# Low halves of the weights from glu to mix, written by accumulating transfers

## The reference

```python
h = rmsnorm_2(x, norm1_g)
z = h @ w_in + b_in
z_glu, z_rx, z_rg, z_ga, z_gb = jnp.split(z, split_idx, axis=-1)
u = z_glu[..., :D_CONV] * jax.nn.sigmoid(z_glu[..., D_CONV:])
u = causal_depthwise_conv(u, conv_dw_w, conv_dw_b)        # 31 taps, 1024 channels
u = jax.nn.silu(layernorm(u, conv_ln_g, conv_ln_b))
y_a = u @ conv_w_out + conv_b_out
xb = causal_depthwise_conv(z_rx, lru_conv_w, lru_conv_b)  # 4 taps, 1280 channels
hb = rg_lru(xb, ...)                                      # gates (two block matrices), then a scan in time
y_b = (hb * jax.nn.gelu(z_rg, approximate=True)) @ lru_w_out
m = jax.nn.sigmoid(z_ga) * y_a + jax.nn.sigmoid(z_gb) * y_b
x = x + m @ w_mix_out
h = rmsnorm_2(x, norm2_g)
x = x + (jax.nn.silu(h @ ffn_w1) * (h @ ffn_w3)) @ ffn_w2
```

## Time and profile before

| | us |
|---|---|
| median of 3 runs | 1075.47 |
| lowest, highest | 1074.18, 1077.63 |
| the profiled execution, its own time | 1070.71 |
| its span, first to last instruction | 1068.8 |
| TensorE matmul busy | 1003.8 (94%) |
| VectorE busy | 788.7 (74%) |
| ScalarE busy | 524.7 (49%) |
| GpSimd busy | 1.9 |

### The profile page before, as it was taken

One profiled execution on the slowest core, in us unless ns is written; L12 is line 12 of the kernel. 1 busy time (PEld: TensorE's weight loads), 2 busy tenths in 40 slices (PEclk: granted clock), 3 DMA queues, 4 the chain that ended last, 5 costly groups with the idle time before them and its releaser, 6 DMA issues.

```text
span 1068.8 us, 20025 instructions
## 1 busy us (share of the span) xinstructions
PE 1003.8 (94%) x7906; PEld 944.9 (88%) x7906; DVE 788.7 (74%) x1449; ACT 524.7 (49%) x823; POOL 1.9 (0%) x14
## 2 busy tenths in 40 slices
PE   4659999999999889999999999999989999999996
PEld 1259999999888779999999989998868999999995
DVE  4477678887767468778766779899995787777554
ACT  3236575444655356666445435457215564444341
POOL 0000000000000000000000000000000000000000
PEclk9679999999999999999999999999999999999998
DMA  9978585888548646555465535363434556555531
GB/s 377 421 319 315 180 313 178 303 329 330 182 124 294 239 161 247 186 173 194 158 223 182 180 108 213 119 236 119 158 118 142 216 174 217 179 179 192 197 119 40
DMA packets 35943, 222.76 MB, mean 208 GB/s; under 512 B 3819, under 2 KB 9116, under 8 KB 9500
## 3 DMA queue, kind: packets, MB, share of 16 engines
q1 hardware_dynamic: 35868, 221.71, 57.8%
HBM read 220.62 MB, written 1.07 MB: 207 GB/s over the span
## 4 chain that ended last, share of the span: by engine, by line
PE 81%; DVE 10%; ACT 3%; DMA 3%; issue 1%; SPq 0%; DVEq 0%; ACTq 0%
PE bank L557 23%; PE bank L559 23%; PE bank L558 23%; PE bank L798 6%; PE bank L848 3%; DVE y L1560 2%; DMA mod_raw<-w_mod 2%; DVE w_lo L1242 1%; PE bank L576 1%; DMA raw<-weights 1%; DVE rt L1623 1%; DMA x<-x_in 0%; PE bank L602 0%; ACT w_hi L909 0%; PE bank L724 0%
## 5 line engine op out<-in xcount | busy, mean ns | idle before, releaser
L557 PE MATMUL bank<-xg_hi,w_hi 128*128 128x258 f32 (+1 forms) x1264 | 360.9, 286 | 4.6 <-DVE w_lo L1242 2.8
L1242 DVE TENSOR_TENSOR w_lo<-raw,w_hi 128x1024 fp32r<-128x1024 f32 x270 | 326.6, 1217 | 45.7 <-ACT w_hi L909 44.8
L558 PE MATMUL bank<-xg_lo,w_hi 128*128 128x258 f32 (+1 forms) x1264 | 356.7, 282 | 0.0
L559 PE MATMUL bank<-xg_hi,w_lo 128*128 128x258 f32 (+1 forms) x1264 | 356.7, 282 | 0.0
L909 ACT ACTIVATE w_hi<-raw 128x1024 fp32r<-128x1024 f32 x270 | 282.3, 1051 | 118.6 <-PE bank L559 105.2
L557 PEld LDWEIGHTS bank<-xg_hi,w_hi 128*128 128x128 f32 x1264 | 239.7, 190 | 7.4 <-issue 4.4
L558 PEld LDWEIGHTS bank<-xg_lo,w_hi 128*128 128x128 f32 x1264 | 240.0, 190 | 0.2
L559 PEld LDWEIGHTS bank<-xg_hi,w_lo 128*128 128x128 f32 x1264 | 239.6, 190 | 0.0
L557 PE MATMUL bank<-hid_hi,w_hi 128*128 128x256 f32 x512 | 142.5, 278 | 1.5 <-DVE ab L1389 1.5
L558 PE MATMUL bank<-hid_lo,w_hi 128*128 128x256 f32 x512 | 142.1, 278 | 0.0
L559 PE MATMUL bank<-hid_hi,w_lo 128*128 128x256 f32 x512 | 142.1, 278 | 0.0
(11 more groups left out here) (214 smaller groups left out, 1329.4 us busy)
## 6 DMA issues: line engine op xcount, KB each, us to landing
raw<-weights SPq DMA_DIRECT2D x157, 1024.0 KB, 5.0
mod_raw<-w_mod SPq DMA_DIRECT2D x32, 1024.0 KB, 9.4
mod_raw<-w_dots SPq DMA_DIRECT2D x16, 1024.0 KB, 8.1
toep<-bias_by_distance SPq DMA_DIRECT2D x8, 256.0 KB, 5.5
x<-x_in SPq DMA_DIRECT2D x1, 1024.0 KB, 5.1
toep<-bias_by_distance SPq DMA_DIRECT2D x8, 128.0 KB, 4.0
y_out<-yout SPq DMA_DIRECT2D x8, 128.0 KB, 1.8
invc<-inv_count SPq DMA_DIRECT2D x1, 512.0 KB, 13.0
```

The lines of the kernel that those rows point to most:

```text
L557: pe.matmul(dst, hi, r_hi, start=start, stop=False, skip_group_check=True)
L558: pe.matmul(dst, hi, r_lo, start=False, stop=False, skip_group_check=True)
L559: return pe.matmul(dst, lo, r_hi, start=False, stop=stop, skip_group_check=True)
L1242: ve.tensor_tensor(w_lo[:, at % HL, :], raw[:, slot, (at % 2) * UT * P:(at % 2 + 1) * UT * P], w_hi[:, at % HL, :].bitcast(F32), ALU.subtr ...
```

## The change

For the units from glu to mix that are split (8 of glu, 10 of rx, 8 of gates, 8 of conv, 8 of mix: 42 units, the list `LOW_BY_DMA`) VectorE no longer subtracts. ScalarE writes the high half and right behind it a second copy with scale -1.0 into `w_lo`, in fp32r as well, that is the negated high half (new semaphore `neg_hi_done`). GpSimd waits for that copy and issues a transfer of the unit from HBM with `accum_op=add` onto `w_lo`, 128 rows of 4096 bytes. One semaphore for each of the 4 slots (`lo_in`) tells that it has landed, and TensorE waits for that in place of `lo_done`. So each of these units is now read from HBM twice.

Three things follow in the text. SyncE waits for `neg_hi_done` of a pair's second unit before it loads over the pair. The units of down1 are written out on ScalarE instead of looped, since the first four units of glu are prepared in it. The scratch for descriptors that GpSimd writes grows from 1024 to 4096 bytes a partition. An old semaphore `neg_done` is renamed. Apart from this the table of taps is new: glu holds 63 steps (51 before), rx and rg 80 (66), gates 32 (30), so 65 are left for gb and ga, where 93 stood.

```diff
+LOW_BY_DMA = [u for u in range(U0["glu"], U0["ffn"]) if u not in NATIVE]
+def low_landed(u):
+    return 16 * sum(n <= u and n % HL == u % HL for n in LOW_BY_DMA)
...
-TAPS_AT = {"glu": [0, 0, 0, 0, 1, 1, 1, 1] + 5 * [7] + 3 * [4],
-           "rx": 5 * [3, 0] + 5 * [4] + 2 * [8] + 3 * [5],
-           "gates": 5 * [3] + 3 * [5],
+TAPS_AT = {"glu": [0, 0, 0, 0, 3, 4, 4, 4] + 8 * [6],
+           "rx": 10 * [3] + 10 * [5],
+           "gates": 8 * [4],
            "gb": [1, 9, 9, 1, 9, 1, 7, 7] + 8 * [6]}
...
+        neg_done = sem("neg_hi_done")
+        lo_in = [sem(f"lo_in{k}") for k in range(HL)]
...
+                elif p >= RAW and 2 * (p - RAW) in LOW_BY_DMA:
+                    sp.wait_ge(neg_done, LOW_BY_DMA.index(2 * (p - RAW) + 1) + 1)
                 elif p >= RAW:
-                    sp.wait_ge(lo_done, splits(2 * (p - RAW) + 1))
+                    sp.wait_ge(lo_done, low_splits(2 * (p - RAW) + 1))
...
+            def low_half(n):
+                at = LOW_BY_DMA[n]
+                pool.wait_ge(neg_done, n + 1)
+                pool.dma_start(w_lo[:, at % HL, :], weights[at // 2, :, (at % 2) * UT * P:(at % 2 + 1) * UT * P].bitcast(F32R),
+                               accum_op=ALU.add).then_inc(lo_in[at % HL], 16)
+            for n in range(HL):
+                low_half(n)
             pool.wait_ge(pe_units, U0["glu"])
             nc.gpsimd.memset(rx[:, :, 0:RTAPS - 1], 0.0).then_inc(pads, 1)
             nc.gpsimd.memset(u[:, :, 0:TAPS - 1], 0.0).then_inc(pads, 1)
+            for n in range(HL, len(LOW_BY_DMA)):
+                low_half(n)
...
                 pe.wait_ge(hi_done, count_of(name, i, j))
-                pe.wait_ge(lo_done, count_of(name, i, j))
+                if isinstance(i, int) and U0[name] + 8 * i + j in LOW_BY_DMA:
+                    pe.wait_ge(lo_in[(U0[name] + j) % HL], low_landed(U0[name] + 8 * i + j))
+                else:
+                    pe.wait_ge(lo_done, low_count(name, i, j))
...
+                if isinstance(i, int) and 8 * i + at in LOW_BY_DMA:
+                    act.activation(w_lo[:, at % HL, :], raw[:, slot, (at % 2) * UT * P:(at % 2 + 1) * UT * P], ACT.Copy,
+                                   scale=-1.0).then_inc(neg_done, 1)
...
-            loop_units(act, "down1", lambda i, j: down("down1", i, j, 3, lambda m: gain1[:, one(m)]))
+            for v in range(32):
+                down("down1", v // 8, v % 8, 3, lambda m: gain1[:, one(m)])
...
-                if isinstance(i, int) and (8 * i + at >= N_UNITS or 8 * i + at in NATIVE):
+                if isinstance(i, int) and (8 * i + at >= N_UNITS or 8 * i + at in NATIVE or 8 * i + at in LOW_BY_DMA):
                     return
...
-    nc = bacc.Bacc("TRN2", target_bir_lowering=False, num_devices=1, dynamic_dma_scratch_size=1024)
+    nc = bacc.Bacc("TRN2", target_bir_lowering=False, num_devices=1, dynamic_dma_scratch_size=4096)
```

16 lines of the change are left out of this document (11 added, 5 removed).

## The result

| | median (lowest to highest) | profiled execution, its span | granted clock |
|---|---|---|---|
| before | 1074.83 (1073.53 to 1077.63) | 1070.71, 1068.8 | 0.974 |
| after | 1129.92 (1127.13 to 1134.12) | 1134.12, 1132.2 | 0.96 |

The ratio is 1.0525, 95% interval 1.0498 to 1.0551. The sign and the place of the loss were as forecast, the size was not: +55 us against +12.4. The profiled execution of after was the longest of its four; that of before, 1070.71 us, is shorter than each of the four timed ones. So the two spans differ by 63.4 us where the medians differ by 55.1.

What follows compares the result with a forecast made beforehand. TensorE, busy 94% of the span, was taken to bound the kernel. A loss of 19.7 us less a gain of 7.3 gave +12.4, on the median 1075.47 said as 1088 us; range for 8 in 10, 1073 to 1102.

Steps and rivals of the forecast that it cites:

- The gain: At lru's start the wait for the layernorm's sum (4.85 us) and slow clock (1.7) go; conv to mix 0.7; 7.3 us.
- Rival 4: At lru the moved taps don't help, since the recurrence ends late by itself; 5 us more, 1093, chance 0.03.
- The way round of a slot and its limits: Room before TensorE waits, glu to mix: glu 2.6 us, rx 4.9 twice, gates 0.3, conv 6.3 and 6.2, mix 6.2 and 4.9.
- D: Time from the end of ScalarE's negated copy to TensorE's release, glu to mix; taken as 7 us odd units, 5 even.
- The price of D: Accumulating transfers, glu to mix: bounded 3.8 to 9.3 us, 7 taken for odd units, 5 for even; loss 19.7 us.
- The three signs: Wrong if landings are under 4.5 us, the raw pair makes no difference, or ScalarE's second copy is much under 1.05 us.
- The load: DMA share 0.63 in rx, 0.81 in gates; with accumulations like 1 MB, gates asks for well over what transfers can do.
- rival 3: Slow accumulation, 8 us or more, or clock stalls; DMA bounds rx and gates; +20 to +30, 1096 to 1105, chance 0.17.
- ScalarE in gates: In gates ScalarE falls behind with the second copies, ending at 723.9 against 719.4 now; limit 0.3 us at unit 7.
- GpSimd's writing of descriptors: On GpSimd's in-order queue, issuing transfers costs nothing while it takes under 3 us.
- SyncE's earlier signal: SyncE's raw pair loads get their signal about 1 us sooner than from VectorE; worth nothing, raw pairs are early.
- Down1's loop: ScalarE's written-out loop in down1 costs nothing, covered by TensorE's work; one or two us if not covered.

Runs made afterwards that it cites:

- before_idle_taps: The kernel before with 12 convolution taps moved from the end of ga into times in which VectorE waits; 1065.93 us, ratio 0.9941.
- thin pairs: The changed kernel with raw pairs loaded over the slots of glu to mix cut to 16 of 2048 columns; 1084.64 us, ratio 1.0106.
- the cast copy: The changed kernel with GpSimd's transfers casting the unit over the negated copy, without the add; 1102.2 us, ratio 1.026.
- half the columns: The changed kernel accumulating only the first 512 of each unit's 1024 columns, on all partitions; 1109.4 us, ratio 1.0333.

## Why the prediction was wrong, by its own steps

- **The gain**, 4.85 + 1.7 + 0.7 = 7.3 us: right in its two large terms. lru gave 6.8; the wait for the sum and the low clock behind it are gone, and before_idle_taps brings most of it by taps alone. The 0.7 us at the turn from conv to mix did not come: TensorE still waits 0.6 us for `act_lo` there, and 0.7 with thin pairs, though no subtraction stands ahead of it any more. Rival 4 is out.
- **The way round of a slot and its limits**: right in kind. With the measured D of the eight places (9.96 at glu 5, 13.17 and 8.81 at rx 5 and 9, 13.54 at gates 7, 11.99 and 11.42 at conv 3 and 7, 9.77 and 9.06 at mix 3 and 7) the same limits give 7.4 + 8.3 + 3.9 + 13.2 + 5.7 + 5.2 + 3.6 + 4.2 = 51.5 us. Measured 62.2. With thin pairs the sum is 12.4 against 19.1, with the cast copy 23.9 against 35.4, with half the columns 31.2 against 42.6, and where the raw pair waits for a landing or the unit comes from SBUF 42.1 against 59.3 and 38.3 against 57.0. It is too low each time, by 7 to 19 us. So a slot's way round, read at eight places, explains two thirds to four fifths of the loss, and the four fifths in the changed kernel are in part luck. The load fits the changed kernel's total just as well, but fails with half of the pairs; the way round underrates the middle of rx, where a sooner issue changed nothing. Both limits hold in the changed kernel at once: D is long because the queues are full, and a long D costs time because there are four slots. I can't divide the 62 us between them.
- **The price of D**: this is the step that failed, the term of the sum that was sized too small. It took 7 us for odd units and 5 for even ones. Measured are 6 us alone, 8 to 10 with one raw pair beside it and 12 to 15 in a backlog. The even units have 10.0 us in the mean and the odd ones 10.8. With D as measured the prediction's own limits give a loss of 51.5 us in place of 19.7. The value came from counting bytes ("the engines that move the data handle as many bytes as for a raw pair"). The lower bound of 3.8 us took 512 KB at the pace of a copy, and even the upper one, 9.3 us, allowed a unit that adds at half the pace of a copy but only one raw pair beside it. A packet with the add takes 0.328 us for 4096 bytes, a plain one 0.325 for 8192. The three signs that it named for being wrong (landings under 4.5 us, no effect of the raw pair, a much cheaper second copy) all lie on the fast side; none of them came.
- **The load.** The prediction said that gates would ask for over all that the transfers can do if an accumulation was as much work as 1 MB, and then put that case into rival 3 at 0.17. It could have been the forecast from the earlier trace rows alone: with 1 MB at 2.2 us for each of ten units, rx asks for 0.63 x 28.3 + 22 = 40 us of the transfers in a stage of 28.3. The sum treated each landing as if the one before it had left the queue empty, and gave no figure for a queue that never empties.
- **Even rival 3 was too small**: it put 20 to 30 us on it. It did name the clock, with two or three places of 1.7 us; it was 17.4 us in five stages. That is more than the 11 us that the sum of the second point lacks, so the two can't simply be added. TensorE waits some 2 us in each unit, and the granted clock is 0.81 in gates, part of the time at 1.2 GHz instead of 2.4.
- **ScalarE in gates** and GpSimd's writing of descriptors: the copies cost 1.04 us, as said, and the issue 0.86, under the 3 us that were allowed. Gates lose 3.5 us with the second copies and no transfers, so ScalarE's own share there is small. SyncE's earlier signal was put at nothing; waiting for the landing instead gives back about 5 us, so it had a small price.
- **Down1's loop** at nothing: right by the median (0.9984 to 1.0028), though its profile looks 3.4 us longer.
- **Small sums**: at D = 8 the prediction's terms add to 27.7 us, not 27. Nothing hangs on it.
- **The estimates from the notes**: the Trainium skill, "DMA: Bandwidth & Descriptors", section on the anatomy of one DMA, gives 2.0 us plus bytes over 436 GB/s, an estimate of 3.2 us for a unit. The runs differ: 5.8 us from issue to landing alone, 9.7 in the median. The Trainium skill, "Collectives: The Full Stack", in its part on why the bus runs under link rate, has the add's two source reads at half rate. The packets come near that, 0.340 us with the add and 0.193 without. The estimate from both, 4.4 us, falls short by 1.4 us even of the landing alone, and it has no queue beside it.

## What to carry to other kernels

A transfer that takes over an engine's work lies on the way round of a buffer. Count that way (buffer left, preparation, issue, landing beside the full load) against buffers less one times the pace of the consumer, and do it for the slowest transfer, not the mean: of four slots one late one is enough. Count its load in time of packets, not in bytes, and look at the share of the queues that the stages have already. And before work is moved to another engine to free time, look whether the wait can be taken away by moving a few operations into that engine's own pauses.
